# A hybrid decoder layer on one core: gates loaded eight tiles at a time, the residual through two small buffers, the last eight tiles' activations kept on chip

## What is computed

```
s = einsum(x @ wq, keys)                       # 8 heads, two halves of 128 keys
sv, si = top_k(s, 16)                          # per head and half
cv, ci = top_k(sv[0][:, None] + sv[1][None, :], 16)
eidx = i1 * 128 + i2                           # 128 experts for a token
gate = softmax(cv)
h = gelu(einsum('tkd,td->tk', u_tab[eidx], x))
out = einsum('tk,tkd->td', gate * h, v_tab[eidx])
y = rmsnorm(hidden + out)
```

## Time and profile before

| | us |
|---|---|
| median of 3 runs | 2089.19 |
| lowest, highest | 2087.47, 2090.67 |
| the profiled execution | 2096.82 |
| its span | 2094.9 |
| TensorE busy | 1909.6 (91%) |
| VectorE busy | 1468.0 (70%) |
| ScalarE busy | 887.9 (42%) |
| GpSimd busy | 771.3 (37%) |
| granted TensorE clock, mean | 0.952 of 2.4 GHz |

### The profile page before, as it was taken

The page is one execution under the profiler, slowest core; times in us unless marked ns, Lnnn a source line. Parts: engine busy times, 40 slices in busy tenths (PEclk is TensorE's granted clock), DMA queues, the critical chain, the costliest instruction groups (busy, mean ns, idle before and its releaser), DMA issues. The chain is left out here.

```text
span 2094.9 us, 29404 instructions
## 1 busy us (share of the span) xinstructions
PE 1909.6 (91%) x11235; PEld 1753.7 (84%) x11235; DVE 1468.0 (70%) x2582; ACT 887.9 (42%) x1768; POOL 771.3 (37%) x438
## 2 busy tenths in 40 slices
PE   5999799696889879899998999999888999989998
PEld 4999698596877679799998999999867888777876
DVE  5878645625513137989999999845477989788885
ACT  3456212114322123344346999844333443343333
POOL 1333151234420032367774555577611222222210
PEclk8999899698999989999999999999989999999999
DMA  4221101115624113289996999999999999999993
GB/s 138 76 76 47 46 1 31 56 41 149 227 97 161 51 55 103 89 294 336 365 374 258 373 372 373 377 395 407 403 344 389 399 400 397 401 370 387 400 397 112
DMA packets 211163, 511.41 MB, mean 244 GB/s; under 512 B 13264, under 2 KB 143056, under 8 KB 174160
## 3 DMA queue, kind: packets, MB, share of 16 engines
q1 hardware_dynamic: 172720, 258.65, 36.2%
q0 software_dynamic: 27648, 201.34, 24.1%
q10 hardware_dynamic: 10656, 49.55, 5.8%
HBM read 450.48 MB, written 59.02 MB: 243 GB/s over the span
## 5 line engine op out<-in xcount | busy, mean ns | idle before, releaser
L1931 POOL TENSOR_TENSOR ex_first_ulo<-ex_first_u,ex_first_uhi 128x1024 fp32r<-128x1024 f32 x127 | 304.9, 2402 | 209.7 <-ACT ex_first_uhi L1962 104.9
L2050 PE MATMUL ps<-xhi,ex_first_uhi 128*128 128x384 f32 x1024 | 352.8, 344 | 9.4 <-PEq L1642 4.9
L2050 PE MATMUL ps<-xhi,ex_first_ulo 128*128 128x384 f32 x1024 | 344.1, 336 | 0.0
L2050 PE MATMUL ps<-xlo,ex_first_uhi 128*128 128x384 f32 x1024 | 344.0, 336 | 0.0
L1556 POOL DMA_INDIRECT ga_ring<-in_uv,ga_idx x138 | 164.0, 1189 | 315.5 <-DVE found L1582 180.1
L2349 PE MATMUL ps<-po_vhi,po_whi 128*128 128x512 f32 x768 | 241.2, 396 | 34.3 <-DVE po_wlo L2382 16.5
L2349 PE MATMUL ps<-po_vlo,po_whi 128*128 128x512 f32 x768 | 238.9, 392 | 0.0
L2349 PE MATMUL ps<-po_vhi,po_wlo 128*128 128x512 f32 x768 | 238.7, 392 | 0.0
L2050 PEld LDWEIGHTS ps<-xhi,ex_first_uhi 128*128 128x128 f32 x1024 | 194.0, 189 | 11.2 <-issue 7.0
L2349 PEld LDWEIGHTS ps<-po_vhi,po_whi 128*128 128x128 f32 x768 | 145.1, 191 | 69.0 <-issue 21.1
L2050 PEld LDWEIGHTS ps<-xlo,ex_first_uhi 128*128 128x128 f32 x1024 | 193.9, 189 | 0.0
(11 more groups left out here) (418 smaller groups left out, 4237.4 us busy)
## 6 DMA issues: line engine op xcount, KB each, us to landing
ex_first_u<-in_uT SPq DMA_DIRECT2D x128, 512.0 KB
scores<-in_peer_v SPq DMA_DIRECT2D x32, 1024.0 KB
po_v<-in_peer_v SPq DMA_DIRECT2D x32, 1024.0 KB
gates<-scores ACTq DMA_DIRECT2D x12, 2048.0 KB
scores<-gates SPq DMA_DIRECT2D x32, 768.0 KB, 16.2
acts<-ex_h ACTq DMA_DIRECT2D x62, 384.0 KB
scores<-acts SPq DMA_DIRECT2D x31, 768.0 KB
in_w_raw<-in_w_in SPq DMA_DIRECT2D x24, 512.0 KB
```

What stands on the lines that cost most here:

```text
L1931: pool.tensor_tensor(ulo[:, j % 3], u[:, j % 3], uhi[:, j % 3].bitcast(F32), ALU.subtract).then_inc(low, 1)
L2050: mm = pe.matmul(ps[:, j % 2, 0:ND], w[:, j % 3, k, :], x[:, k, :], start=(k == 0 and n == 0), stop=(k == KT - 1 and n == 2))
```

## The change

The change has five parts.

1. Gates are loaded for eight tiles at once: 16 loads of 1536 KB with pieces of 1024 bytes, in place of 32 loads of 768 KB with pieces of 512. The second buffer (`po_g`) is new.
2. The second table now begins with the last eight tiles (120 to 127), whose activations all stay in SBUF. Two stores and one load of activations fall away.
3. The residual comes in four parts through two buffers of two blocks: loads at steps 5, 7, 25 and 27, additions after tiles 16, 20, 36 and 40. The sample tokens' part is one load, at step 11.
4. From tile 92 on (`VECTOR_LOW`) VectorE makes `ulo`, not GpSimd. In VectorE's order it stands ahead of the pick of the step before. GpSimd then only issues gathers.
5. All four tiles of the first group are multiplied with their gates before the barrier. Some small tiles share memory (`act` with `dot`, `y3` with `gather.x`).

```diff
+VECTOR_LOW = FIRST_SPREAD + QUADS // PER_STEP + 2
...
-        self.g = flat[:, 8 * ND:16 * ND].rearrange("p (s k b t) -> p s k b t", s=2, k=ND // 32, b=4)
+        self.g = flat[:, 8 * ND:16 * ND].rearrange("p (k b t) -> p k b t", k=ND // 32, b=8)
...
     def load_w(self, sp, io, i):
         for c in range(2):
-            sp.wait_ge(self.h_stored[c], 16 * i)
-        sp.dma_start(self.w[:, i % 2], io["acts"][i - 1]).then_inc(self.w_loaded[i % 2], 16)
-
-    def load_g(self, sp, io, i):
-        q = (i - 1) % (NKEY // 4)
-        sp.dma_start(self.g[:, i % 2], io["gates"].rearrange("k p e t -> p k e t")[:, :, 4 * q:4 * q + 4, :]
-                     ).then_inc(self.g_loaded[i % 2], 16)
...
+            sp.wait_ge(self.h_stored[c], 16 * (i - 1))
+        sp.dma_start(self.w[:, i % 2], io["acts"][i - 2]).then_inc(self.w_loaded[i % 2], 16)
+
+    def load_g(self, sp, io, m, g):
+        c = (8 * m - 8) % NKEY
+        sp.dma_start(g, io["gates"].rearrange("k p e t -> p k e t")[:, :, c:c + 8, :]
+                     ).then_inc(self.g_loaded[m % 2], 16)
...
-            output.load_g(sp, io, 0)
-            sp.dma_start(output.v[:, :, :], io["peer_v"].rearrange("(p e) d -> p e d", p=P)[:, NKEY - 4:NKEY - 2, :]
+            output.load_g(sp, io, 0, output.g)
+            sp.dma_start(output.v[:, :, :], io["peer_v"].rearrange("(p e) d -> p e d", p=P)[:, NKEY - 8:NKEY - 6, :]
                          ).then_inc(output.v_loaded[0], 16)
-            output.load_w(sp, io, 1)
-            output.load_g(sp, io, 1)
...
-                if j + 2 < NKEY and not 0 <= x < QUADS // PER_STEP:
+                if j + 2 < VECTOR_LOW and not 0 <= x < QUADS // PER_STEP:
                     rest(j + 2)
...
-                if j % 2 == 0 and 0 < j <= NKEY - 4:
+                if j % 2 == 0 and 0 < j <= NKEY - 8:
...
+            dve.wait_ge(low, VECTOR_LOW)
+            lows = VECTOR_LOW
+
+            def rest(j):
+                dve.wait_ge(high, j + 1)
+                dve.wait_ge(products, j - 2)
+                dve.tensor_tensor(ulo[:, j % 3], u[:, j % 3], uhi[:, j % 3].bitcast(F32), ALU.subtract
+                                  ).then_inc(low, 1)
+
             for n in range(LOOP_PICKS - LATE, LOOP_PICKS):
+                while lows < min(pick_step(n) + 2, NKEY):
+                    rest(lows)
+                    lows += 1
                 pick(n)
...
             dve.wait_ge(output.g_loaded[0], 16)
-            dve.wait_ge(gelus, NKEY - 1)
-            output.weigh(dve, 0, 0, 3).then_inc(output.weighted, 1)
+            dve.wait_ge(gelus, NKEY - 4)
+            output.weigh(dve, 0, output.g)
...
-        ADD_H = 16
+        LOAD_H = [5, 7, 25, 27]
+        ADD_H = [16, 20, 36, 40]
...
+            for c in range(2):
+                sp.wait_ge(first.h_stored[c], 16 * (NKEY // 4 - 2))
             load_v(2)
+            first.load_g(sp, io, 1, gs[1])
             for e in range(NKEY):
...
+                if e % 8 == 4 and e // 8 + 2 < GROUPS // 2:
+                    m = e // 8 + 2
+
+                    sp.wait_ge(weighted, 2 * m - 2)
+                    first.load_g(sp, io, m, gs[m % 2])
```

More of the change, by code:

```diff
@@ L2203, in _ @@
                     pick(EARLY + q // PER_STEP)
+            dve.wait_ge(low, VECTOR_LOW)
[5 more added lines that the diff above has]
+                                  ).then_inc(low, 1)
             for n in range(LOOP_PICKS - LATE, LOOP_PICKS):
+                while lows < min(pick_step(n) + 2, NKEY):
+                    rest(lows)
+                    lows += 1
                 pick(n)
+            for j in range(lows, NKEY):
+                rest(j)
             for n in range(LOOP_PICKS - 2, LOOP_PICKS):
@@ L2227, in peer_output @@
         whi = sb("whi", [P, 2, 4, ND], F32R)
-        hC = sb("hC", [P, KT, HC])
+        hC = sb("hC", [P, 2, 2, ND])
+        hS = sb("hS", [P, KT, NS])
+        g_late = sb("g", [P, ND // 32, 8, 32])
+        gs = [first.g, g_late[:, :, :, :]]
         wlo = sb("wlo", [P, 2, 4, ND], F32R)
         acc_s, gain = found.place[:, 0:D], found.place[:, D:2 * D]
-        y3 = sb("y3", [P, D])
+        y3 = gather.x[:, 0, :]
         stat = sb("stat", [P, 3, 5])
         v_loaded, hg_loaded, gg_loaded = first.v_loaded, first.w_loaded, first.g_loaded
-        h_loaded, gain_loaded = sem("po_h_loaded"), sem("po_gain_loaded")
+        h_loaded, gain_loaded = [sem(f"po_h_loaded{i}") for i in range(2)], sem("po_gain_loaded")
+        hS_loaded, h_added = sem("po_hS_loaded"), sem("po_h_added")
         weighted = first.weighted
@@ L2266, in load_w @@
                 first.load_w(sp, io, q)
-                first.load_g(sp, io, q)
+            for c in range(2):
+                sp.wait_ge(first.h_stored[c], 16 * (NKEY // 4 - 2))
             load_v(2)
+            first.load_g(sp, io, 1, gs[1])
             for e in range(NKEY):
[L2271 to L2277, removed]
+                if e in LOAD_H:
+                    r = LOAD_H.index(e)
+                    if r >= 2:
+                        sp.wait_ge(h_added, r - 1)
+                    sp.dma_start(hC[:, r % 2], io["saved"][:, 2 * r:2 * r + 2, 0:ND]).then_inc(h_loaded[r % 2], 16)
+                if e == 11:
+                    sp.dma_start(hS[:, :, :], io["saved"][:, :, SEQ:NT]).then_inc(hS_loaded, 16)
                 if e == 19:
@@ L2355, in _ @@
                     mm.then_inc(products, 1)
[L2356 to L2357 removed]
+                if e in ADD_H:
+                    r = ADD_H.index(e)
+                    pe.wait_ge(h_loaded[r % 2], 16 * (r // 2 + 1))
                     for t in range(DT):
[L2359 to L2361 removed]
+                        for k in range(2 * r, 2 * r + 2):
+                            mm = pe.matmul(ps[:, 2 * t + k // 4, (k % 4) * P:(k % 4 + 1) * P],
+                                           hC[:, r % 2, k % 2, t * P:(t + 1) * P], ident, start=False, stop=False,
+                                           skip_group_check=True)
+                    mm.then_inc(h_added, 1)
             pe.wait_ge(gather.summed, NPICK)
             pe.wait_ge(normed, 1)
+            pe.wait_ge(hS_loaded, 16)
             for a in range(2):
@@ L2399, in scale @@
                                          in1=gain[0:n, :], op0=ALU.mult, op1=ALU.mult).then_inc(normed, 1)
-            first.weigh(dve, 0, 3, 4).then_inc(weighted, 1)
             rest(0)
```

38 lines of the change are left out of this document (17 added, 21 removed).

## The result

The changed kernel is slower: 2130.64 us (median of 4 runs, 2126.18 to 2143.50) against 2089.93 (4 runs, 2087.47 to 2092.38), a ratio of 1.0213 with a 95% interval of 1.0187 to 1.024. The forecast was 2073.2, and the measured time lies outside the range. The profiled execution took 2126.18 us, its span is 2124.3.

The account below looks back on a forecast made before the run. `po_v` loads at the full DMA were taken to hold back TensorE in the second table; TensorE bounded the first table's end. Terms -15 + 1.5 - 2.5 = -16.0 us gave 2080.8 profiled, 2073.2 median; own range 2065 to 2082, wider 2062 to 2087.

Parts of the forecast that it names:

- the new order of SyncE's list: Second table: in every second group the pair of `v` stands behind 0.79 MB more, 3.6 us; 2 us counted as uncovered.
- the rival with 4%: Second table: 15 double loads delay a pair by 3.6 us each, 54 us, early ones give nothing back; 2122 us, 4%.
- The price of a piece: Second table's gate loads: 1024 bytes cost 50 ns against 31 for 512, saving 17.3 us of DMA time; bounds 0 and 44.6.
- The start: Second table behind the barrier: the double load of gates stands ahead of the third pair, with no slack; 2.5 us lost.
- VectorE's `ulo`: First table: `ulo` moved from GpSimd fits in VectorE's wait for gathers in one written order; +1.5 us counted.
- The barrier: TensorE's gap between tables: last gather leaves up to 4.9 us earlier; gain of 2.5, bounds gain 4.9 and loss 1.
- The marks: Signs of success: second table's TensorE idle below 6 us, clock 1.00, DMA share below 1.03, shorter `po_v` wait, gap near 14.
- The mark on packets: Second table's DMA queues: fewer packets under 2 KB, about half of 51,539, as a sign of success.

Follow-up runs that it names:

- e1: Changed kernel with each eight-tile gate load cut into two halves of six token blocks, one per group of four tiles, pieces still 1024 bytes: 2073.17 us.
- e10: Changed kernel, double loads kept, with a third buffer for a pair of v and the residual through one small buffer: 2073.41 us.
- e2: As e1, but each gate load is cut by tiles (four of eight each), so pieces are 512 bytes: 2089.86 us.
- e8: e1 with the first load of gates behind the barrier moved behind the third pair of v: 2068.02 us.
- e4: Changed kernel with part 4 alone undone, so GpSimd makes `ulo` for all tiles again: 2137.05 us.
- e5: Kernel before with part 4 alone added, so VectorE makes `ulo` from tile 92 on: 2084.02 us.
- e3: Changed kernel with the double load of gates issued two steps later, behind its group's `po_v` pair and ahead of the other buffer's: 2121.45 us.
- e12: e1 with a third buffer for a pair of v as well: 2070.51 us.

## Why the prediction was wrong

**The step that failed** is the one on the new order of SyncE's list: "`vhi` and `vlo` hold four tiles, so one late load is covered if the one before was early; I put 2 us on what isn't covered". The runs put it at 57 (e1 and e10). Its price stood in the prediction, as the rival with 4%: 15 loads by 3.6 us, 54 us, nothing given back. The measured 57.5 are 3.8 for each of 15 periods. That the two numbers are so near is in part luck, because the rival priced the delay alone: in the profiled executions the stage of the changed kernel is 62.5 us longer than e1's, of which 40.9 are TensorE's added idle time, 2.7 a period, and 21.6, 1.4 a period, are the same matmuls at a lower clock (0.96 and 0.99). What was wrong was the cover. Four tiles of `vhi` and `vlo` are a cover only if they can be filled ahead, and nothing can be: a pair is loaded when its buffer's `vlo` are made, and the rounds had no slack, as the prediction itself read from rows 2 and 3 (a load of over 12 us makes the round longer than TensorE's group, and ScalarE waited in 29 of 32). A late pair then delays its own reload. An early one gains nothing, since the next issue waits for VectorE. The weight against this rival, "four tiles of `vhi` and `vlo`", was space, not time ahead.

**The price of a piece** was right: 12 ns a pair and 17.3 us for the stage were forecast, 14 ns and 16.7 us of the whole time measured (22.1 between the stages of single executions). By the Trainium skill's rule on the smallest transfer at line rate ("DMA: Bandwidth & Descriptors", section "Specifications") it would have been nothing; e1 against e2 doesn't agree with it.

**The start** was put at 2.5 us; e1 against e8 gives 2.6 in the stage and 5.2 in the medians, neither clear of the spread. The 26 matmuls more in the first 40 us are 5.9 us at the 0.227 each of the earlier trace rows, so 2.5 was rather low.

**VectorE's `ulo`** was put at +1.5: TensorE is busy 149.00 of 149.00 us in the first table's end and makes 861 matmuls where it made 860, so it cost nothing. The 1.2 us in the wait for a gather were indeed free there.

**The barrier** was put at -2.5 between -4.9 and +1; the gap fell by 6.4, beyond the bound, of which part 4 alone gives 4.6. I had taken the barrier to keep its distance from a last gather that leaves earlier. Against the end of the first table that gather left only 1.6 us earlier (7.2 us ahead of it, and not 5.6), but the barrier opened 14.0 us behind it and not 18.7. The step that was missed is that the gathers now come one by one:

```profile
1484.06 0.94 POOL L1556 DMA_INDIRECT hT<-in_uv,ga_idx  x1 [1.80 <-DVE ps L1582]
1492.34 0.94 POOL L1556 DMA_INDIRECT ga_ring<-in_uv,ga_idx  x1 [7.35 <-DVE ps L1582]
```

Before, three left within 5 us behind the two last `ulo`, at 1501.45, 1505.22 and 1506.47; in e4, without part 4, three again, and the barrier opened 17.8 us behind the last. The packets show what that changes. The last packet of the gathers' queue lies 13.2 us behind the last issue before (1519.7), 12.4 in e4, but 8.9 in the changed kernel (1501.2). From that packet to SyncE's first load behind the barrier it is 5.1 to 5.5 us in all fourteen kernels of this document, while the last packet of SyncE's own queue lies 2.8 to 6.6 us ahead of that load. So the barrier keeps its distance from the landing of the last gather, not from its issue. Nothing in the rows names what releases it.

**The marks** did their work: the second table's DMA share fell below 1.03, which was put down as a sign of success. It was one only if TensorE became busier, and 0.94 at 362 GB/s with a TensorE that is idle for 46 us is the sign of the opposite. The mark on packets came true (26,425 under 2 KB, where it was 51,539) and said nothing of the time. In e1, where the relief came, the share is 0.98 with more GB/s, 389.

**What adds up, and what doesn't.** e2, with pieces of 512 bytes and even halves, takes as long as the kernel before; from e2 to e1 the pieces give 16.7, and from e1 to the changed kernel the double loads take 57.5, +40.8 against the measured 40.7. These are differences of neighbouring runs, so that they must add up; they test nothing. e2's zero has parts of its own: its gap at the barrier is 5.2 us shorter than before, and its second table 8.0 us longer, 11.5 longer than that of e5. The start accounts for 2.6 to 5.9 of that. The rest lies in parts 2 and 3, in the gates' larger buffers or in the spread of single executions; none of these was tried by itself.

**Still open.** Why e3 gives back 9.2 us and not nothing. In e3 only the double load of 1.57 MB stands between two pairs, where in the changed kernel the activations stand there too, 2.36 MB together; no run separates that. And e10 changes more than the number of buffers: its pairs are issued two steps earlier in SyncE's list, and the residual goes through one buffer at other steps. e12 against e1, within 3 us, shows that the residual's new steps cost little. e3 shows that a place in the list alone gives little, not that it gives nothing.

## What to carry to other kernels

Merging two loads into one that is twice as large halves the number of transfers, but it also makes a queue's list uneven. Price the burst by what stands behind it on that queue. Count as cover only work that can really be fetched ahead: here that was set by the number of buffers for the delayed operand, not by the number of tiles that its consumers hold. And add what a lower clock takes behind the waits, here a third of the loss in the stage (21.6 of 62.5 us). Larger pieces and an even list don't exclude each other: splitting the merged load along the other dimension kept the pieces of 1024 bytes and gave the 17 us. When a kernel gets slower and the DMA share falls with it, look for the moments at which the queues run dry.

## What the runs showed of the hardware

- An issue behind many small pieces can hold SyncE. In the changed kernel the pair behind a double load of 1536 pieces took 3.24 us at 1654.13 and 5.85 at 1614.41 to issue, where most take 0.33. The runs point to the number of pieces rather than the bytes: with 768 KB of gates ahead of it, the issue of the `po_v` pair has a median of 2.14 us in the kernel before (1536 pieces of 512 bytes, 30 issues from 1530 to 2045) and of 0.33, at most 0.50, in e1 (768 pieces of 1024 bytes). In e2, again with 1536 pieces of 512, it is 0.63, at most 7.00.

```profile
1614.41 5.85 SPq L2279 DMA_DIRECT2D po_v<-in_peer_v  x1
```

- Pieces of 1024 bytes are not yet at the rate of large ones. By the saving of 14 ns a pair one takes an estimated 48 ns (2 x 31 - 14), 21 MB in a millisecond of one engine, against 16 for 512 bytes and 26 for 8 KB.
- The barrier opens 5.1 to 5.5 us behind the last packet of the gathers, in all fourteen kernels. Behind the issue of the last gather that is 17.8 and 18.7 us where three leave within 5 us (e4, before), and 13.5 to 15.2 in the other twelve.
